# Forgetting attention taken by pairs of heads, its result written by feature

## The reference, cut to what matters

```python
c = jnp.cumsum(log_f, axis=1).transpose(0, 2, 1)
for blk in range(s // Q_BLOCK):                       # Q_BLOCK = 128, s = 256: two blocks of queries
    q0, q1 = blk * Q_BLOCK, (blk + 1) * Q_BLOCK
    logits = jnp.einsum('bhqd,bhkd->bhqk', q[:, :, q0:q1], k[:, :, :q1]) * d ** -0.5
    logits = logits + c[:, :, q0:q1, None] - c[:, :, None, :q1]
    causal = jnp.arange(q0, q1)[:, None] >= jnp.arange(q1)[None, :]
    prob = jax.nn.softmax(jnp.where(causal, logits, -jnp.inf), axis=-1)
    outs.append(jnp.einsum('bhqk,bhkd->bhqd', prob, v[:, :, :q1]))
...
h = h + jnp.concatenate([o_g, o_f], axis=-1) @ w_out[i]
```

## Time and profile before

| what | value |
|---|---|
| median of 3 runs | 840.09 us (839.66 to 842.61) |
| the profiled execution's own time | 840.55 us |
| its span | 838.5 us |
| PE busy | 796.8 us (95%) |
| DVE, ACT, POOL busy | 512.4, 386.8, 96.8 us |
| stage of the six levels | from about 504.7 to 575.7 us of the span |

### The profile page before, as it was taken

The page is one execution under the profiler, slowest core; times in us unless marked ns, Lnnn a source line. Parts: engine busy times, 40 slices in busy tenths (PEclk is TensorE's granted clock), DMA queues, the critical chain, the costliest instruction groups (busy, mean ns, idle before and its releaser), DMA issues. The chain is left out here.

```text
span 838.5 us, 12695 instructions
## 1 busy us (share of the span) xinstructions
PE 796.8 (95%) x5135; PEld 711.6 (85%) x5135; DVE 512.4 (61%) x686; ACT 386.8 (46%) x527; POOL 96.8 (12%) x162
## 2 busy tenths in 40 slices
PE   4899999999799999999999999999999999999996
PEld 3578777777699999987789988988799999988885
DVE  0374789866685666685577884454464554554364
ACT  3433413544565555524367545546364344343373
POOL 3010221311100000000160314110000000000000
PEclk9899999999999999999979999999999999999999
DMA  9936577723166646587633342211455565555521
GB/s 327 382 127 216 170 258 261 274 78 100 51 201 201 196 159 193 170 291 247 200 104 102 125 131 97 102 51 55 146 189 182 172 199 184 168 175 194 182 101 50
DMA packets 102445, 142.74 MB, mean 170 GB/s; under 512 B 6263, under 2 KB 62080, under 8 KB 102400
## 3 DMA queue, kind: packets, MB, share of 16 engines
q1 hardware_dynamic: 96688, 138.42, 49.2%
q10 hardware_dynamic: 5648, 3.69, 1.5%
q0 software_dynamic: 64, 0.01, 0.0%
HBM read 141.05 MB, written 1.05 MB: 169 GB/s over the span
## 5 line engine op out<-in xcount | busy, mean ns | idle before, releaser
L1797 PE MATMUL ps<-h_hi,w_hi 128*128 128x256 f32 x720 | 204.5, 284 | 0.9 <-DVE w_lo L1180 0.9
L1798 PE MATMUL ps<-h_lo,w_hi 128*128 128x256 f32 x720 | 203.7, 283 | 0.0
L1799 PE MATMUL ps<-h_hi,w_lo 128*128 128x256 f32 x720 | 203.7, 283 | 0.0
L1180 DVE TENSOR_TENSOR w_lo<-raw,w_hi 128x2048 fp32r<-128x2048 f32 (+1 forms) x62 | 137.5, 2226 | 64.9 <-ACT w_hi L640 64.6
L640 ACT CAST w_hi<-raw 128x2048 fp32r<-128x2048 f32 (+1 forms) x62 | 114.9, 1856 | 88.2 <-PE ps L1799 53.2
L1797 PEld LDWEIGHTS ps<-h_hi,w_hi 128*128 128x128 f32 x720 | 138.2, 192 | 1.1 <-DVE w_lo L1180 1.1
L1188 DVE TENSOR_TENSOR w_lo<-raw,w_hi 128x2048 fp32r<-128x2048 f32 x44 | 100.8, 2290 | 61.6 <-ACT w_hi L648 61.6
L1798 PEld LDWEIGHTS ps<-h_lo,w_hi 128*128 128x128 f32 x720 | 138.2, 192 | 0.0
L1799 PEld LDWEIGHTS ps<-h_hi,w_lo 128*128 128x128 f32 x720 | 138.2, 192 | 0.0
L648 ACT CAST w_hi<-raw 128x2048 fp32r<-128x2048 f32 x44 | 83.6, 1900 | 50.6 <-PE ps L1799 50.6
L1797 PE MATMUL ps<-w_hi,h_hi 128*128 128x512 f32 x200 | 81.1, 405 | 1.2 <-DVE h_lo L1203 0.7
(11 more groups left out here) (384 smaller groups left out, 1251.3 us busy)
## 6 DMA issues: line engine op xcount, KB each, us to landing
raw<-in_ffn_up_w SPq DMA_DIRECT2D x22, 1024.0 KB, 5.1
raw<-in_w_gate_up SPq DMA_DIRECT2D x22, 1024.0 KB, 5.1
raw<-in_ada_w SPq DMA_DIRECT2D x16, 1024.0 KB, 5.3
raw<-in_w_in SPq DMA_DIRECT2D x14, 1024.0 KB, 5.3
raw<-in_m_in_w SPq DMA_DIRECT2D x11, 1024.0 KB, 5.2
raw<-in_ffn_down_w SPq DMA_DIRECT2D x10, 1024.0 KB, 5.1
raw<-in_w_down SPq DMA_DIRECT2D x10, 1024.0 KB, 5.0
raw<-in_m_out_w SPq DMA_DIRECT2D x4, 1024.0 KB, 5.3
```

What stands on the lines that cost most here:

```text
L1180: dve.tensor_tensor(part_view(w_lo, s), raw_view(split[s]), part_view(w_hi, s).bitcast(F32), ALU.subtract).then_inc(lo_ready, 1)
L1797: pe.matmul(dst, l_hi, r_hi, start=first, stop=False)
L1798: pe.matmul(dst, l_hi, r_lo, start=False, stop=False)
L1799: return pe.matmul(dst, l_lo, r_hi, start=False, stop=last)
```

## The change: what it does

The 8 heads are taken as 4 pairs. Logits of both heads of a pair are issued in turn, head 0 on rows 0 to 63 of the array into bank 0, head 1 on rows 64 to 127 into bank 1. Mask, maximum, exponential and division work on a pair; the division now comes before the transposition, on the probabilities (`fox_normed`), and the scale goes into the copy of q out of PSUM. The product with the values is turned round: the values (64 columns) are the stationary operand, so the output has features on the partitions, head 0 in partitions 0 to 63, head 1 in 64 to 127 of bank 2. It is split straight into `fox_hi` and `fox_lo` (ACT, DVE), and `mix_pair` is left with the delta rule's half. `mix` shares `vb`, and `fox_hi`, `fox_lo` share the place of `qk_n`.

The order becomes (T: transposition, L: logits, O: product with the values, of pair 0 to 3): L0 ahead of the levels; level 0: T0 at its end; level 1: O0, L1 ahead of `y_mm`, T1 at its end; level 2: O1; level 3: L2 ahead of the transpositions, T2 at its end; level 4: L3 ahead of the transpositions, O2; level 5: T3 ahead of `y_mm`, O3 behind it.

```diff
-FOX_STEPS = ((1, None), (2, None), (3, 4), (5, 6), (7, 8), (9, None))
# GpSimd
-            def fox_mask(h):
-                pool.wait_ge(S("logit_ready"), TT * (h + 1))
-                for c in (0, 2 * P):
-                    keep(logit[:, h % 2, c:c + P], ALU.is_ge, [[-1, P]], 1, fill=NEG).then_inc(S("logit_masked"), 1)
+            def fox_mask(i):
+                pool.wait_ge(S("logit_ready"), i + 1)
+                blocks = logit[:].rearrange("p h (a n) -> p h a n", n=P)
+                for a in (0, 2):
+                    keep(blocks[:, :, a, :], ALU.is_ge, [[0, 2], [-1, P]], 1, fill=NEG).then_inc(S("logit_masked"), 1)
...
+            level_of(2)
+            fox_mask(1)
+            level_of(3)
+            level_of(4)
+            fox_mask(2)
+            level_of(5)
+            fox_mask(3)
# ScalarE: fox_evac scales q and no longer runs hi_until(s + 4) for m >= 2
+            def fox_exp(i):
+                act.wait_ge(S("fox_max"), i + 1)
+                for h in range(2):
+                    for t, part in ((0, slice(0, P)), (1, slice(P, 3 * P))):
+                        act.activation(logit[:, h, part], logit[:, h, part], ACT.Exp, bias=row_max[:, t, h:h + 1],
+                                       accum_out=row_sum[:, t, h:h + 1]).then_inc(S("prob2_ready"), 1)
+            def prT_out(i):
+                act.wait_ge(S("prT_mm"), i + 1)
+                act.copy(prT[:], ps[:, 0:2, 0:3 * P]).then_inc(S("prT_ready"), 1)
+            def fox_hi_out(i):
+                act.wait_ge(S("fox_mm"), i + 1)
+                if i == 0:
+                    act.wait_ge(S("k_dec_ready"), 1)
+                act.copy(fox_hi[:, i, :], ps[:, 2, 0:T]).then_inc(S("fox_hi_ready"), 1)
# VectorE
+            def fox_normed(i):
+                dve.wait_ge(S("prob2_ready"), 4 * (i + 1))
+                link(dve.reciprocal(fsum[:, 1, :], fsum[:, 1, :]))
+                for t, part in ((0, slice(0, P)), (1, slice(P, 3 * P))):
+                    ins = dve.tensor_tensor(logit[:, :, part], logit[:, :, part],
+                                            row_sum[:, t, :].unsqueeze(2).to_broadcast([P, 2, (t + 1) * P]), ALU.mult)
+                ins.then_inc(S("rows_normed"), 1)
...
+            fox_logits(0)
+            fox_max(0)
+            update(0)
+            fox_normed(0)
+            lo_until(at["fox_v"][0] + 4)
+            fox_logits(1)
+            fox_lo_out(0)
+            fox_max(1)
+            update(1)
+            fox_normed(1)
+            lo_until(at["fox"][2] + 3)
# TensorE
+                for t, part, keys in ((0, slice(0, P), slice(0, P)), (1, slice(P, 3 * P), slice(0, T))):
+                    for h in range(2):
+                        row = slice(FD * h, FD * h + FD)
+                        ins = pe.matmul(ps[:, h, part], foxT[row, i, t * P:(t + 1) * P], foxT[row, FP + i, keys],
+                                        start=True, stop=True)
...
+                for s in range(TT):
+                    for h in range(2):
+                        c = slice((2 * i + h) * FD, (2 * i + h + 1) * FD)
+                        ins = pe.matmul(ps[FD * h:FD * h + FD, 2, s * P:T], fox_v[:, s, c], prT[:, h, 2 * P * s:2 * P + s * P],
+                                        start=s == 0, stop=s == 1)
...
-            mix_pair(0)
-            mix_pair(1)
```

More of the change, by code:

```diff
@@ L943, in fox_evac @@
                 act.wait_ge(group_used, s + 1)
-                act.copy(foxT[:, 2 * j:2 * j + 2, :], ps[:, m if m < 2 else 3, :].rearrange("p (f t) -> p f t", f=2))\
-                    .then_inc(S("fox_T"), 2)
-                hi_until(s + 4)
+                act.activation(foxT[:, 2 * j:2 * j + 2, :], ps[:, m if m < 2 else 3, :].rearrange("p (f t) -> p f t", f=2),
+                               ACT.Copy, scale=FD ** -0.5 if j < 2 else 1.0).then_inc(S("fox_T"), 2)
+                if m < 2:
+                    hi_until(s + 4)
             def bank_out(dst, bank, want, func=None):
@@ L1047, in _ @@
                     bank_out(invT[:, GH * t:GH * (t + 1), :].rearrange("p h t -> p (h t)"), 6 + t, "turned")
[L1048 to L1052, removed]
+                if i == 0:
+                    fox_exp(0)
+                    v_out(1)
+                    prT_out(0)
+                elif i == 1:
+                    fox_hi_out(0)
+                    fox_exp(1)
+                    fox_evac(2)
+                    prT_out(1)
+                elif i == 2:
+                    fox_hi_out(1)
+                    fox_evac(3)
+                elif i == 3:
+                    fox_exp(2)
+                    z_out(0)
+                    prT_out(2)
+                elif i == 4:
+                    fox_hi_out(2)
+                    fox_exp(3)
+                    z_out(1)
+                else:
+                    prT_out(3)
             act.wait_ge(S("u_mm"), 1)
@@ L1062, in mix_hi @@
                 act.wait_ge(S("tr"), base("tr", "mix") + i + 1)
[L1063 to L1071, removed]
+                dst, src = h_hi[:, 2 * i:2 * i + 2, :], ps[:, 4 + i, :].rearrange("p (f t) -> p f t", f=2)
+                act.activation(dst, src, ACT.Copy, scale=pcol("gdn_norm", 0)).then_inc(S("hi"), 1)
+            fox_hi_out(3)
             act.wait_ge(S("st_mm"), 1)
@@ L1668, in fox_step @@
[L1668 to L1679, removed]
-            A0 = at["att_out"][0]
[L1681 to L1704, removed]
@@ new lines, in fox_lo_out, with update @@
+            def fox_lo_out(i):
+                dve.wait_ge(S("fox_hi_ready"), i + 1)
+                lo_part(fox_lo[:, i, :], ps[:, 2, 0:T], fox_hi[:, i, :], "fox_done")
+            def update(i):
+                for t in range(TT):
+                    dve.wait_ge(S("y_mm"), TT * i + t + 1)
+                    if i < len(LEVELS) - 1:
+                        ins = dve.tensor_tensor(all_heads(inv, t), all_heads(inv, t), bank(6 + t), ALU.subtract)
+                    else:
+                        ins = dve.tensor_tensor(all_heads(invT, t), all_heads(invT, t), bank(4 + t), ALU.subtract)
+                    ins.then_inc(S("inv_ready"), 1)
@@ new lines, in _ @@
+            A0 = at["att_out"][0]
+            fox_logits(0)
[9 more added lines that the diff above has]
+            lo_until(at["fox"][2] + 3)
+            fox_lo_out(1)
+            update(2)
+            lo_until(at["fox"][3] + 3)
+            fox_logits(2)
+            fox_max(2)
+            update(3)
@@ L1706, in mix_lo @@
+            fox_normed(2)
+            lo_until(at["z"][0] + 3)
+            fox_logits(3)
+            fox_max(3)
+            fox_lo_out(2)
+            update(4)
+            fox_normed(3)
+            lo_until(A0 + 2)
+            update(5)
             def mix_lo(i):
                 dve.wait_ge(S("hi"), base("hi", "mix") + i + 1)
[L1709 to L1715, removed]
@@ L2417, in _ @@
+                ins.then_inc(S("fox_mm"), 1)
+            fox_logits(0)
             for t in range(TT):
@@ L2461, in _ @@
                     between[i]()
-                if FOX_STEPS[i][1] is not None:
-                    fox_step(FOX_STEPS[i][1])
+                if i in (0, 1, 3):
+                    fox_transpose((i + 1) // 2)
+            fox_out(3)
             for t in range(TT):
```

136 lines of the change are left out of this document (62 added, 74 removed).

## The result

| | before | after |
|---|---|---|
| median of 6 runs | 842.39 us (839.66 to 844.84) | 835.98 us (833.72 to 838.12) |
| ratio of the times | | 0.9921 (95% interval 0.9891 to 0.995) |
| span of the profiled execution | 838.5 us | 836.4 us |
| from the first matmul of the value projection to the first of `att_out(0, 0)`, "the stage" below | 499.13 to 581.93: 82.80 us | 503.94 to 579.87: 75.93 us |

The kernel became 0.8% faster, 6.6 us by the ratio, where 6.0 had been forecast; 835.98 stands against the forecast median of 834.2 and lies in its range. The median of before over these six runs is 2.3 us above the one that was known, so the ratio is the better measure.

What follows compares the result with a forecast made beforehand. PE's issued work plus few waits was taken as the bound; gains of 4.96 + 0.2 + 0.8 = 5.96, say 6.0 us, from 840.55 gave 834.6, median 834.2; 8-in-10 range 832.8 to 838.0.

Steps and rivals of the forecast that it cites:

- What a pair costs: On PE: logits 0.85 us and product 0.85 with heads side by side, 1.51 each if serial; transpositions 0.76.
- Levels 0 to 4: Steps and a wait of 13.09 us removed, 7.38 added, new waits of 0.45 and 0.3: 4.96 us gained.
- the wait at T1: In level 1, pair 1's chain of 8.05 us against 7.60 of cover: PE waits 0.45 us (0 to about 1.2).
- the wait in level 3: Between the transpositions and `y_mm`, PE waits for ACT's copy: 0.3 us (0 to 0.8).
- Level 5: From `z_tile(1)`'s end to `u`: ACT sets `y_mm`'s start, 4.2 to 4.4 us after the projection; 0.2 us gained (-0.2 to 0.4).
- The tail: Behind level 5: eight transpositions go (0.87 us), a later state copy costs PE 0.1; 0.8 us gained.
- A: Rival: row halves run one after the other, strips of columns together; gain 4.0 us, time 836.1; chance 0.10.
- B: Rival: row halves and column strips both run serially; gain 1.6 us, time 838.5; chance 0.08.
- C: Rival: a pair's chain is longer (masks, divisions or POOL's hold); 1.0 us more gives 835.4, 1.7 gives 836.8; chance 0.12.
- D: Rival: the pair's chain so long it eats the gain, beyond 2.9 us more; 844.9 at 4.5 more; chance 0.05.
- E: As forecast, but no wait at T1 or in level 3: 0.75 us more gained, 833.4; chance 0.65 together with the forecast.
- The wait of 0.82: In level 2 PE waits 0.82 us for ACT's projection copy before head 4's logits; counted as removed in full.

Runs made afterwards that it cites:

- the same rows: The changed kernel with both heads of a pair taking their logits from rows 0 to 63: stage 77.82 us, ratio to before 0.9944.
- the same strip: The changed kernel with both heads' products written to partitions 0 to 63, one head after the other: stage 78.31 us, ratio to before 0.9944.
- the late split: The changed kernel with ACT's split of att_out's third weight group moved behind the copies of level 5: stage 74.94 us, ratio to before 0.9912.

## Why the prediction was right

**What a pair costs.** L forecast 0.85, measured 0.86; O 0.85, measured 0.80; both at the end taken, and the other end, 1.51, is what the same rows (1.50) and the same strip (1.44) cost. The reading behind it, pitch by column plus 0.19 for going to 64 rows and back, fits: serial is 1.32 + 0.18, so the extra comes once for a visit and not once for a head. For O the extra is 0.14. What the extra is made of no run took apart. The transpositions were put at 0.76 and took 0.66, 0.71 and 0.66: in the kernel before each three were followed by a product of another shape, and whether that made the difference was not tested.

**Levels 0 to 4.** From the start of the value projection to the transposition in level 5 it was 568.19 - 499.13 = 69.06 us, and the part that answers to it is 567.39 - 503.94 = 63.45: 5.61 gained, forecast 4.96. The difference is a sum of small terms: the wait at T1 (0.05 where 0.45 stood, 0.4), three transpositions (0.25), three O (0.15), less three L (-0.03) and the wait in level 3 (0.45 where 0.3 stood, -0.15); 0.62 of the 0.65.

**The wait at T1.** This is the term that was furthest off, and it lies in the range that stood beside it (0 to 1.2). The chain was put at 8.05 us and took 7.63: masks 0.77 for 0.9, maxima and negation 2.36 for 2.45, reciprocal and division 1.24 for 1.35, the rest in the adds, the exponentials and the signals. The cover was 7.60 as forecast (523.71 to 531.35), so chain and cover meet within 0.05 us. The negation under POOL's product was foreseen for pair 1, not for pairs 0 and 2. That it costs PE no more than 0.1 us is shown by moving the product, and that it can cost a great deal by the kernel before with its logits moved. The other transpositions had their cover: the divisions end 2.05, 1.14 and 4.37 us ahead of T0, T2 and T3, where about 2, about 0.7 and over 4 were forecast.

**Level 5.** Forecast 0.2, measured: 568.19 to 575.66 before is 7.47, 567.39 to 574.48 after is 7.09, so 0.38. `y_mm` starts 4.19 us after the projection (forecast 4.2 to 4.4), and `u` 2.90 behind it, to the hundredth as before. That ACT sets this start is shown by the late split, by which alone `y_mm` comes 0.87 us earlier; the prediction had put its wait near 0.9.

**The tail.** 575.66 to 581.93 was 6.27, 574.48 to 579.87 is 5.39: 0.88 for the 0.8 forecast.

5.61 + 0.38 + 0.88 = 6.87 in place of 5.96. PE's busy time in the stage fell by 6.2 us (80.97 to 74.81) where about 7 was forecast for the whole kernel; on the page it fell by 3.3 only, as PE was busy 2.8 us longer ahead of the stage. The later stages kept their time. Rivals A and B are out by experiment; C and D would have shown idle time ahead of T1, and there is none. E, no wait at T1 nor in level 3, is half true. The wait of 0.82 was counted as a gain of its own. It is gone, but the kernel before, with its logits moved, only exchanged it for longer ones: it could not be had alone by that move, and the prediction's sum took it at its full length with no word on what it would release. In the changed kernel L2 stands a level behind the projection that it needs, and the negation of pair 1, held too, has cover.

The median, 835.98, is 1.8 us above the forecast though the stage gained 0.9 more. The forecast started from a median of 840.09, and over six runs the kernel before had 842.39: those 2.3 us, less the 0.65 that were gained beyond the forecast, are nearly all of it. What lies ahead of the stage spreads by some us from run to run, and in the two profiles much of that lies in stretches at the lower granted clock; what sets where these fall was not tested. So the ratio and the stage bear the prediction out, and the median less so.

## What to carry to other kernels

Where PE is the bound, take small matmuls two at a time: here a pair took 0.86 us on two halves of the rows, in different banks, and 0.80 us on two strips of 64 columns, where it takes 1.50 and 1.44 us without the sharing, and the order of the heads made no difference. By the reading above, fewer visits to a small shape also save its price of 0.14 to 0.19 us each. Before a wait is removed, follow what is released earlier because of it: in the kernel before, a POOL product that started 0.85 us earlier came ahead of a tiny operation on DVE and held it for its own length. And count a new idle time of PE, where it is as long as the 2.2 and 3.3 us here, together with the matmuls behind it, which ran at about half the clock.

## What the runs showed of the hardware that was not expected

- Two heads issued one after the other, on different rows or strips, took the same time as issued in turn (L 0.86 and 0.86, O 0.81 and 0.80).
- An idle time of 3.30 us cost another 2.70 in slower matmuls, at a granted clock of 0.50; idle times of 1.80 and 0.36 us close together cost another 1.62, at 0.53. At the single waits of up to 0.87 us of the two kernels the stage kept its clock of 1.00.
- A negation of two numbers a partition took 0.17 us, or 2.28 us when it started 0.09 us behind a POOL product of 1024 columns; started 0.53 us ahead of such a product, it took 0.17.
